# A two-block model kernel: the loads, transposes and squares of the opening are regrouped

## What is computed

```python
def rmsnorm(x, w):
    y = x * lax.rsqrt(jnp.mean(x * x, axis=-1, keepdims=True) + EPS)
    return y * w

def gla_mixer(hn, w_in, w_gate_up, b_gate, out_norm, w_out):
    proj = jnp.einsum('btd,de->bte', hn, w_in)          # 2048 x (1024 + 1024 + 2048 + 2048 + 32)
    q, k, v, og, lr = jnp.split(proj, ...)              # lr: 2 x 16 columns, the low-rank gate input
    gk = einsum('btzr,zrd->zbtd', lr, w_gate_up) + b_gate
    logdec = log_sigmoid(gk) / 16
    ...                                                 # chunked gated linear attention, both directions
    return einsum('bte,ed->btd', rmsnorm(o, out_norm) * silu(og), w_out)

h = x + gla_mixer(rmsnorm(x, mixer_norm), ...)
h = h + swiglu(rmsnorm(h, ffn_norm), ...)
...                                                     # per-layer embedding, final norm
second_block(h, ...)                                    # a conv + mLSTM branch and a pooling branch, merged
```

## Time and profile before

| | us |
|---|---|
| median of 3 runs | 2307.2 |
| lowest and highest | 2304.74, 2307.3 |
| the profiled execution's own time | 2304.34 |
| its span | 2302.2 |
| PE busy in it | 2256.7 (98%) |
| DVE, ACT, POOL busy | 1289.2, 1054.8, 40.9 |
| mean DMA rate | 180 GB/s |

### The profile page before, as it was taken

How to read it: one execution, slowest core, us unless ns; L and a number is a source line. 1 busy time by engine, 2 the same in 40 slices (tenths; PEclk the granted TensorE clock), 3 DMA queues, 4 the chain that set the end, 5 groups by cost and what they waited for, 6 DMA issues and landing times.

```text
span 2302.2 us, 27398 instructions
## 1 busy us (share of the span) xinstructions
PE 2256.7 (98%) x10271; PEld 1858.0 (81%) x10271; DVE 1289.2 (56%) x1555; ACT 1054.8 (46%) x1356; POOL 40.9 (2%) x43
## 2 busy tenths in 40 slices
PE   6999999999999999999999998999999999999997
PEld 5788888888888888888878877888888888888886
DVE  3677755555555445545546564777555556545554
ACT  4464444444444334444445544444445554443443
POOL 0000000000000000000000120000000000000000
PEclk9999999999999999999999999999999999999999
DMA  6564466666566666656656654656655556666553
GB/s 203 160 177 131 125 203 184 188 187 191 186 189 189 186 191 192 189 186 191 187 165 202 187 154 161 189 175 196 191 176 169 166 167 186 194 193 210 184 192 101
DMA packets 283093, 413.89 MB, mean 180 GB/s; under 512 B 21309, under 2 KB 145993, under 8 KB 282473
## 3 DMA queue, kind: packets, MB, share of 16 engines
q1 hardware_dynamic: 280976, 406.32, 57.9%
q10 hardware_dynamic: 2010, 6.12, 0.8%
HBM read 410.28 MB, written 2.10 MB: 179 GB/s over the span
## 4 chain that ended last, share of the span: by engine, by line
PE 80%; issue 17%; DVE 1%; ACT 1%; DMA 0%; ACTq 0%; POOL 0%; POOLq 0%; DVEq 0%
PE acc L906 25%; PE acc L908 25%; PE acc L907 25%; PE tp L922 2%; PE mx L1030 1%; PE tp L1041 1%; PE mx L1057 1%; DVE w_lo L1173 0%; PE mx L986 0%; DMA vec_raw<-in_qk_conv_b 0%; ACT junk L568 0%; ACT xa_hi L560 0%; PE mx L1052 0%; DVE OUT L1677 0%; DVE xa_lo L1190 0%
## 5 line engine op out<-in xcount | busy, mean ns | idle before, releaser
L1173 DVE TENSOR_TENSOR w_lo<-raw,w_hi 128x1024 fp32r<-128x1024 f32 (+3 forms) x788 | 949.2, 1210 | 798.0 <-ACT w_hi L546 797.2
L546 ACT CAST w_hi<-raw 128x1024 fp32r<-128x1024 f32 (+3 forms) x788 | 805.2, 1027 | 922.7 <-PE acc L908 912.1
L906 PE MATMUL acc<-w_hi,xa_hi 128*128 128x512 f32 x2240 | 884.4, 395 | 4.2 <-DVE w_lo L1173 2.8
L908 PE MATMUL acc<-w_hi,xa_lo 128*128 128x512 f32 x2240 | 872.7, 390 | 0.0
L907 PE MATMUL acc<-w_lo,xa_hi 128*128 128x512 f32 x2240 | 872.0, 389 | 0.0
L906 PEld LDWEIGHTS acc<-w_hi,xa_hi 128*128 128x128 f32 x2240 | 420.9, 188 | 92.8 <-issue 4.1
L908 PEld LDWEIGHTS acc<-w_hi,xa_lo 128*128 128x128 f32 x2240 | 420.5, 188 | 88.6
L907 PEld LDWEIGHTS acc<-w_lo,xa_hi 128*128 128x128 f32 x2240 | 421.1, 188 | 85.2 <-issue 1.0
L906 PE MATMUL acc<-w_hi,xb_hi 128*128 128x512 f32 (+1 forms) x400 | 155.1, 388 | 4.3 <-DVE w_lo L1173 4.3
L908 PE MATMUL acc<-w_hi,xb_lo 128*128 128x512 f32 (+1 forms) x400 | 154.0, 385 | 0.0
L907 PE MATMUL acc<-w_lo,xb_hi 128*128 128x512 f32 (+1 forms) x400 | 153.9, 385 | 0.0
(11 more groups left out here) (211 smaller groups left out, 1095.4 us busy)
## 6 DMA issues: line engine op xcount, KB each, us to landing
raw<-in_w_in SPq DMA_DIRECT2D x192, 512.0 KB, 4.2
raw<-in_ffn_w_in SPq DMA_DIRECT2D x352, 256.0 KB, 2.9
raw<-in_gla_w_in SPq DMA_DIRECT2D x96, 512.0 KB, 3.8
raw<-in_ffn_w_out SPq DMA_DIRECT2D x88, 512.0 KB, 3.7
raw<-in_w_in SPq DMA_DIRECT2D x128, 256.0 KB, 3.0
raw<-in_gla_w_out SPq DMA_DIRECT2D x32, 512.0 KB, 4.2
raw<-in_ple_w_gate SPq DMA_DIRECT2D x32, 512.0 KB, 4.2
raw<-in_w_proj_mlstm SPq DMA_DIRECT2D x32, 512.0 KB, 3.9
```

What stands on the lines that cost most here:

```text
L546: nc.scalar.copy(w_hi[:, hl, 0:kc * job.w], raw[:, slot, 0:kc * job.w]).then_inc(hi_ready, 1)
L906: nc.tensor.matmul(a[t][:, 0:w], xh, hi, start=first, stop=False)
L908: ins = nc.tensor.matmul(a[t][:, 0:w], xl, hi, start=False, stop=last)
L1173: nc.vector.tensor_tensor(w_lo[:, hl, 0:kc * job.w], raw[:, slot, 0:kc * job.w], w_hi[:, hl, 0:kc * job.w].bitcast(F32), ALU.subtract) \
```

## The change

What it does, in the order of the program:

- ACT issues one load only, `mixer_norm` into `gain_raw`. PE turns it by one transpose, DVE copies 16 columns into `vec`.
- x is transposed into all eight PSUM banks one after the other (`X_BANKS`), without a wait for a bank to be read. ACT and DVE follow bank by bank.
- `lr` is one granule of 16 k tiles: one transfer of 256 KB in rows of 128 bytes, one split on ACT and one on DVE (after bank 4 of x), and 48 matmuls. Each pair of k tiles waits for `x_split`.
- The squares of x stand in the first `qk` tile: token tile 0 on ACT, token tile 1 on DVE, one each after the splits of granules 0 to 3.
- `wgu`, the masks (now int8 in DRAM, doubled there) and `diag2` are issued by SP after granules 4 and 5 of the first `qk` tile; the other nine vector loads after granule 7, behind a wait for the squares and the transposes, since they land in the space of `H`. PE turns them after granule 5 of the first `v` tile, DVE copies them at granule 7. POOL's two casts are gone.

```diff
@@ plan
-        Job("lr", 1, full, 2 * RANK), Job("qk", 4, full), ...
+        Job("lr", 1, granules(16, 16), 2 * RANK), Job("qk", 4, full), ...
...
+        X_BANKS = [acc[0][0], acc[0][1], mx[0], mx[1], acc[1][0], acc[1][1], tp[0], tp[1]]
@@ block.sync
+            def constants_after(j):
+                if j == 4:
+                    sp.dma_start(wgu[0:RANK, :, :], gla_w_gate_up[0].rearrange("z r d -> r z d")) \
+                        .then_inc(loads["wgu"], 16)
+                    sp.dma_start(wgu[RANK:RANK + 1, :, :], gla_b_gate).then_inc(loads["wgu"], 16)
+                if j == 5:
+                    sp.dma_start(masks[:, :, :], c_masks.rearrange("p (a i) -> p a i", a=7)) \
+                        .then_inc(loads["masks"], 16)
+                    sp.dma_start(diag2[:, :], c_diag).then_inc(loads["diag"], 16)
+                if j == 7:
+                    sp.wait_ge(squared, SQ["x"] + 4)
+                    sp.wait_ge(squared_too, 4)
+                    sp.wait_ge(x_turned, 8)
+                    sp.dma_start(vec_raw[:, 0, :], conv_w[0].rearrange("w (f p) -> (w f) p", p=P)) \
+                        .then_inc(loads["vec"], 16)
...
@@ block.gpsimd
-            pool.wait_ge(loads["masks"], 16)
-            for t in range(2):
-                nc.gpsimd.tensor_copy(masks[:, :, t * P:(t + 1) * P], masks_raw[:, :, :]) \
-                    .then_inc(masks_ready, 1)
@@ block.scalar
+                if name == "qk" and n == 0 and j < 4:
+                    squares(SQ["x"] + j, ssq[:, 0, 0, j:j + 1], H[:, 0, cols(j)])
...
-            for j in range(HL_SLOTS):
-                split_hi(J["lr"], 0, j, 0)
-            act.wait_ge(tp_read[1], 1)
-            for r in range(4):
-                xt_high("x", r, lambda b: 4 * r + 2 * b, lambda k: vcol("mixer_norm", k), 2)
-            for n in range(4):
-                act.wait_ge(x_landed[n], 16)
-                for t in range(2):
-                    squares(SQ["x"] + 2 * n + t, ssq[:, 0, t, n:n + 1], H[:, t, cols(n)])
+            act.dma_start(gain_raw[:, :], mixer_norm[0].rearrange("(f p) -> f p", p=P)).then_inc(loads["gain"], 16)
+            act.wait_ge(gain_ready, 1)
+            for i in range(8):
+                act.wait_ge(x_turned, i + 1)
+                for f in range(2):
+                    ins = nc.scalar.activation(xa_hi[:, 2 * i + f, :], X_BANKS[i][:, f * T:(f + 1) * T], ACT.Copy,
+                                               scale=vcol("mixer_norm", 2 * i + f))
+                ins.then_inc(xt_hi, 1)
+                if i == 4:
+                    split_hi(J["lr"], 0, 0, 0)
@@ block.tensor
+                    if job.name == "lr" and k % 2 == 0:
+                        pe.wait_ge(x_split, k // 2 + 1)
...
+            def vectors():
+                r = J["vec"].r0
+                pe.wait_ge(loads["vec"], 16 * 9)
+                bank(r, 0)
+                nc.tensor.transpose(tp[0][:, 0:P], vec_raw[:, 0, :], ident[:, :])
...
+                if (name, n, j) == ("v", 0, 5):
+                    vectors()
...
+            for i in range(8):
+                if i % 2 == 0:
+                    pe.wait_ge(x_landed[i // 2], 16)
+                if X_BANKS[i] is tp[1]:
+                    pe.wait_ge(gain_ready, 1)
+                for f in range(2):
+                    for t in range(2):
+                        ins = nc.tensor.transpose(X_BANKS[i][:, f * T + t * P:f * T + (t + 1) * P],
+                                                  H[:, t, (2 * i + f) * P:(2 * i + f + 1) * P], ident[:, :])
+                ins.then_inc(x_turned, 1)
@@ block.vector
+                if name == "qk" and n == 0 and j < 4:
+                    if j:
+                        dve.wait_ge(squared_too, j)
+                    nc.vector.scalar_tensor_tensor(out=junk2[:, :], in0=H[:, 1, cols(j)], scalar=1.0,
+                                                   in1=H[:, 1, cols(j)], op0=ALU.mult, op1=ALU.mult,
+                                                   accum_out=ssq[:, 0, 1, j:j + 1]).then_inc(squared_too, 1)
+                if name == "qk" and n == 0 and j == 4:
+                    dve.wait_ge(squared_too, 4)
+                    mean_square(0, SQ["x"] + 4)
...
+                if (name, n, j) == ("v", 0, 7):
+                    vectors()
```

More of the change, by code:

```diff
@@ L63, in plan @@
     jobs = [
-        Job("lr", 1, full, 2 * RANK), Job("qk", 4, full), Job("v", 4, full), Job("og", 4, full),
+        Job("lr", 1, granules(16, 16), 2 * RANK), Job("qk", 4, full), Job("v", 4, full), Job("og", 4, full),
         Job("wo", 4, full),
@@ L92, in plan @@
         byname[name].r0, byname[name].x0 = r, x
-        r, x = r + n, x + 2 * n * split
+        r, x = r + (n if name != "x" else 0), x + 2 * n * split
     return jobs, byname
@@ L256, in build @@
         loads = {k: sem(f"load_{k}") for k in (
-            "ident", "vec", "masks", "diag", "wgu", "xagain", "p", "fn", "windows", "gbias",
+            "ident", "gain", "vec", "masks", "diag", "wgu", "xagain", "p", "fn", "windows", "gbias",
             "npw", "out")}
@@ L448, in load @@
                         .then_inc(landed[slot], 16)
+            def constants_after(j):
[13 more added lines that the diff above has]
+                        .then_inc(loads["vec"], 16)
+                    at_row = GAIN_ROWS
+                    for ap in (gla_out_norm, ffn_norm, ple_norm, final_norm, norm_pre, pool_scale, mlstm_norm):
+                        flat = ap if len(ap.shape) == 1 else ap[0]
+                        n = flat.shape[0] // P
+                        sp.dma_start(vec_raw[at_row:at_row + n, 1, :], flat.rearrange("(f p) -> f p", p=P)) \
+                            .then_inc(loads["vec"], 16)
+                        at_row += n
+                    sp.dma_start(vec_raw[0:32, 2, :], conv_b[0].rearrange("(f p) -> f p", p=P)) \
+                        .then_inc(loads["vec"], 16)
             for job in JOBS:
@@ L463, in _ @@
                             load(job, n, j, n)
+                            if (job.name, n) == ("qk", 0):
+                                constants_after(j)
             for n in range(4):
@@ L656, in evacuate_transposed @@
                 elif name == "og":
+                    for b in range(2):
+                        act.wait_ge(tp_read[b], J["vec"].r0 + 1)
                     xt_high("y", n, lambda b: 4 * n + 2 * b, lambda k: vcol("gla_out_norm", k % 4), 2)
@@ L855, in column_tile @@
                     for j in range(job.G):
-                        if not (job.name == "lr" and j < HL_SLOTS):
+                        if job.name != "lr":
                             split_hi(job, n, j, ns)
@@ L963, in transposes @@
                         ins.then_inc(tp_ready, 1)
+            def vectors():
[3 more added lines that the diff above has]
+                nc.tensor.transpose(tp[0][:, 0:P], vec_raw[:, 0, :], ident[:, :])
+                nc.tensor.transpose(tp[0][:, P:P + 32], vec_raw[0:32, 2, :], ident[0:32, 0:32]).then_inc(tp_ready, 1)
+                bank(r, 1)
+                nc.tensor.transpose(tp[1][:, 0:VEC_ROWS], vec_raw[0:VEC_ROWS, 1, :],
+                                    ident[0:VEC_ROWS, 0:VEC_ROWS]).then_inc(tp_ready, 1)
             def lr_back():
@@ L1130, in _ @@
             pe.wait_ge(loads["ident"], 16)
[L1131 to L1138 removed]
+            pe.wait_ge(loads["gain"], 16)
+            nc.tensor.transpose(tp[1][:, 0:GAIN_ROWS], gain_raw[:, :], ident[0:GAIN_ROWS, 0:GAIN_ROWS]) \
+                .then_inc(gain_turned, 1)
+            for i in range(8):
[8 more added lines that the diff above has]
+                ins.then_inc(x_turned, 1)
             for job in JOBS:
@@ L1427, in gla_place @@
                 else:
+                    if h == 0 and i == 0:
+                        dve.wait_ge(loads["masks"], 16)
                     nc.vector.copy_predicated(
```

81 lines of the change are left out of this document (32 added, 49 removed), and 2 rows, old and new, of the table r.

## The result

The changed kernel takes 2288.97 us (median of four executions, 2286.73 to 2291.03), against 2306.59 (four, 2304.74 to 2307.3) of the kernel before on the same chip: a ratio of 0.9928, 95% interval 0.9916 to 0.994. The profiled execution took 2288.7 with a span of 2286.9. The forecast was 2289, range 2284 to 2295, so size and sign were right. Not every term was.

A forecast was written before the change was run, and what follows sets the result against it. PE was taken as the bound from the first `qk` matmul on: 16.6 us off its start, 0.2 off that matmul, 0.35 paid for vector transposes, in sum -16.5 us; forecast median 2289 us, range 2284 to 2295.

The forecast's parts named there:

- The bound, and that S carries the end: PE never stands from 36.94 to 1190 us, so an earlier first `qk` matmul (start S) shortens the end equally.
- Loads and transposes: Opening: x's first part lands at 5.45 us, transposes start at 5.5, bank 0 is turned at 6.6.
- ACT's table load: Opening on ACT: 1.28 us behind the wait for bank 0, 6.6 to 7.9, a new cost on the path.
- ACT and DVE by bank: Opening: ACT takes 0.85 us a bank, DVE follows 0.89 behind; the low-rank product starts at 13.8.
- The lr weights: Opening: the 256 KB land at 10.9 to 12.9 us, needed at 12.2; no wait taken, bounds 0 and 0.7.
- late weights: Opening: low-rank weights land at about 15 us, S 22.8, 2.5 us more, 2291.5; chance 0.13.
- The product: Low-rank product, 48 matmuls: ten at the low clock level, 38 at the high, 6.5 us, so S 20.3.
- the rival that was given 0.2: Low-rank product at the high clock from its start: 1.1 us less, 2288; chance 0.2.
- Squares: First `qk` tile: squares hidden behind PE at cost 0, DVE's fourth ending near 24 us.
- SP: Nine small loads take 5.3 us; second tile's first granule issued at 29, with 6 us of slack.
- The rival on the other side: Second `qk` tile starves behind SP's wait, costing from issue after about 37 us; 2311 us, chance 0.015.
- The vector transposes: First `v` tile: three transposes on a full PE cost 0.35 us, bounds 0.3 and 0.5, without a wait.

The follow-up runs named there:

- early_table: Changed kernel plus one dummy single-element ACT copy ahead of its waits, so the table load comes earlier; median 2285.7 us, ratio 0.9916.
- after: The changed kernel itself, as profiled and measured; median 2288.97 us, ratio 0.9928 to the kernel before.
- warm: Changed kernel plus thirteen PE transposes of the identity ahead of x's, results unused; profiled span 2285.2 us.
- u_banks: Changed kernel with x again turned through two PSUM banks in turn, each waited for; profiled span 2292.0 us.
- vec_twice: Changed kernel with three more vector transposes in the first `v` tile, results unused; profiled span 2285.8 us.
- sp_hold: Changed kernel where SP also waits for seven used granules ahead of the nine vector loads; profiled span 2291.9 us.
- fill: early_table plus 28 and 18 unused PE transposes of the identity in the two late waits; 2284.2 us, ratio 0.9904.
- after_again: The changed kernel measured once more with no edit; median 2288.7 us, ratio 0.993.
- combo: Changed kernel plus early table load, 13 identity transposes, `lr` weights issued before x's last part and split after bank 3; median 2288.53 us, ratio 0.9929.
- u_lr8: Changed kernel with the low-rank weights again in eight granules instead of one; profiled span 2288.9 us.

## Why the prediction was right, by its steps

*The bound, and that S carries the end.* Right. PE never stands between S and 1180 us; the late waits for `w_lo` are 10.7 us in all (10.9 before) and moved along.

*Loads and transposes.* Transposes start at 5.87 (5.5 said), the first bank is turned at 7.07 (6.6), since x's first part landed 0.4 us later than in the earlier trace rows.

*ACT's table load.* Right in place and size: 7.07 to 8.35, nothing beside it; early_table bought 1.1 to 1.4 us back.

*ACT and DVE by bank.* From start to start ACT took 0.71 to 0.72 and DVE 0.78 to 0.79, where 0.85 and 0.89 were taken from a chain in which a bank stood by itself; the split of `lr` stood at 11.94 (12.2 said), and the product at 13.97 (13.8). The late start and the faster banks cancel.

*The lr weights.* Landed at 11.25, inside 10.9 to 12.9; no wait. The rival "late weights" is out.

*The product.* This term was mis-sized: 6.5 said, 5.48 measured, 48 matmuls at 0.113. The likeliest case took ten at the low level from the pattern of before; what came was the rival that was given 0.2. Its ground was in the text, seven microseconds of PE without a gap, but these were transposes, and the trace of before had shown none that raised the clock. By the Trainium skill, page "TensorE: Matmul & The Clock Gate", part 4 (PE-mode transpose), transposes don't count as work for the clock, so they couldn't. Rows of after and warm say otherwise: nothing but transposes ran before 11.5 us (after) or 6.9 us (warm), and there their duration falls from 421 to 273 ns. That page's rule is not borne out here for float32 transposes; the rows list them as MATMUL and don't show whether the mode that the page means is on. The level isn't certain even so: u_banks, warm and vec_twice had 6, 14 and 15 low matmuls in it.

*Squares.* Hidden, as said: the `qk` splits kept ahead of PE, DVE's fourth square ended at 23.3 (24 said). Undone, they cost 3.7 us of S.

*SP.* The rival on the other side had the right mechanism and nearly the right threshold, 37 us against the 35.7 estimated from sp_hold. Its first load was issued at 27.04 (29 said), as nine issues took 3.7 us and not 5.3:

```profile
23.33 0.34 SPq L468 DMA_DIRECT2D vec_raw<-in_qk_conv_w  x1
...
27.04 3.25 SPq L452 DMA_DIRECT2D raw<-in_gla_w_in  x6
```

*The vector transposes.* 0.35 said with bounds of 0.3 and 0.5; measured 0.46 to the next matmul and 0.1 more in its first spacings, 0.5 to 0.6 in all. Priced from the row of eight transposes of one shape, the three of different shapes came out too cheap.

*The sum.* The text named as a sign against itself that the span shrinks by less than S, and it did: 17.5 off S, 15.3 off the span. Of the 2.2 us, 0.5 is the transposes, -0.15 the first `qk` matmul, and 1.8 are nine more matmuls at the low level at the late places. This was missing from the sum and from the rivals: the earlier trace rows were read as waits that "move along", and nobody asked what the clock does behind a wait of 3.5 us. So the forecast hit the median to 0.1 us partly by luck: the product came 1.0 us shorter than said, the late places cost 1.8 more, and the forecast difference was 16.5 us where the profiles differ by 15.6 and the medians by 17.6. Each median, and the level that the forecast started from, is a middle over executions with more or fewer of these matmuls; how many the unprofiled ones had is not shown.

## What to carry to other kernels

When one engine is the bound, undo the opening's parts one at a time and read the start of the bound engine's steady work, not the end: of four profiles of this opening three agree within 0.3 us (the fourth shows the clock as its reason), while the whole time moves by 4 to 6. Look behind every long wait of TensorE for matmuls at half pace, since the wait's price in the profile leaves them out; work without a use, put into the wait, took both the loss and the spread away. And bringing an operation forward that nobody waits for, as warm did with x's transposes, buys nothing.

## What the runs showed of the hardware

- Transposes of 128x128 in float32 took 421 ns and then 273 ns at the higher level of the clock, and transposes alone brought the change about, in after and in warm. In fill, 28 and 18 of them kept it up through two waits.
- After PE had stood 3.5 us at the first late place, its clock was at the low level for 7 to 13 matmuls in ten profiles, and for none in after_again, warm and vec_twice, with the same wait. At the second place, after 2.4 us, for 8 or 9 in six profiles and for none in the others. What decides it from execution to execution stays open.
- SP's issue next behind the transfer of 256 KB in 2048 rows took 5.89 us (4.89 in combo), others 0.5. In u_lr8, with the same bytes in eight transfers, no one of the eight issues took over 1.3 us:

```profile
L452 SPq DMA_DIRECT2D raw<-in_gla_w_in x6: 469/544/5887, 3.3 to 11.4; - x6
```

```profile
L452 SPq DMA_DIRECT2D raw<-in_gla_w_in x8: 474/620/1312, 3.3 to 8.7; - x8
```

  The first row is after's, the second u_lr8's. In after nobody waited for it.
